# A two-layer diffusion step in float32r pairs: sixteen first places for the modulation pieces, output weights asked for within attention, squares ahead of the fifth piece at the norms, and one more burst in the input projection

## The reference, cut to what matters

```python
sm, cm, gm, sf, cf, gf = split(silu(cond) @ mod_w[l] + mod_b[l], 6)   # per-channel vectors
h = rms_norm(x, g_pre) * (1 + cm) + sm
z = h @ w_in[l]                                   # 2048 -> 4608
o = attention A (6 heads), attention B (6 heads), chunk gMLP (4 groups), all from z
x = x + gm * rms_norm(o @ w_out[l], g_post)       # 2048 -> 2048
h = rms_norm(x, g_pre2) * (1 + cf) + sf
x = x + gf * rms_norm((silu(h @ w_gate) * (h @ w_up)) @ w_down, g_post2)   # 5632 wide
```

## Time and profile before

| | us |
|---|---|
| median of 3 runs | 2378.92 (2378.73 to 2380.59) |
| the profiled execution's own time | 2373.86 |
| its span | 2372.1 |
| PE busy in it | 2276.7 (96%) |
| DVE busy | 1625.2 (69%) |
| ACT busy | 985.3 (42%) |
| POOL busy | 69.2 (3%) |

### The profile page before, as it was taken

The page is one execution under the profiler, slowest core; times in us unless marked ns, Lnnn a source line. Parts: engine busy times, 40 slices in busy tenths (PEclk is TensorE's granted clock), DMA queues, the critical chain, the costliest instruction groups (busy, mean ns, idle before and its releaser), DMA issues.

```text
span 2372.1 us, 27970 instructions
## 1 busy us (share of the span) xinstructions
PE 2276.7 (96%) x10686; PEld 1798.4 (76%) x10686; DVE 1625.2 (69%) x1739; ACT 985.3 (42%) x1277; POOL 69.2 (3%) x97
## 2 busy tenths in 40 slices
PE   4999989999999999999999999899999999999998
PEld 1776766678878888788777887687888888878886
DVE  2555563389888889889887997557888545444455
ACT  2333343364444444334346334347444444433443
POOL 1000120000000000000000101000000000000000
PEclk8999999999999999999999999999999999999999
DMA  8899979868878878788865896865877665666664
GB/s 311 293 348 331 331 246 348 307 209 303 283 254 292 289 263 292 245 282 283 298 225 199 306 320 232 302 200 189 277 261 261 198 194 188 192 179 194 192 219 149
DMA packets 269317, 609.91 MB, mean 257 GB/s; under 512 B 19116, under 2 KB 19296, under 8 KB 267840
## 3 DMA queue, kind: packets, MB, share of 16 engines
q1 hardware_dynamic: 264832, 589.37, 73.1%
q0 software_dynamic: 4352, 18.76, 2.1%
HBM read 603.79 MB, written 5.45 MB: 257 GB/s over the span
## 4 chain that ended last, share of the span: by engine, by line
PE 85%; DMA 7%; DVE 4%; issue 2%; ACT 2%; POOL 1%; SPq 1%; POOLq 0%; DVEq 0%; ACTq 0%
PE bank_B L846 39%; PE bank_A L846 38%; DMA mraw<-in_mod_w 5%; PE bank_X L932 2%; PE bank_M L904 2%; PE bank_M L893 1%; DVE wlo L1441 1%; DMA raw<-in_w_out 1%; ACT whi L1153 1%; PE bank_T L924 1%; DMA raw<-in_w_in 1%; ACT junk L1167 0%; SPq L554 0%; DMA raw<-in_w_gate 0%; DVE x L1549 0%
## 5 line engine op out<-in xcount | busy, mean ns | idle before, releaser
L1441 DVE TENSOR_TENSOR wlo<-raw,whi 128x1024 fp32r<-128x1024 f32 x724 | 880.5, 1222 | 610.8 <-ACT whi L1153 609.8
L1153 ACT CAST whi<-raw 128x1024 fp32r<-128x1024 f32 x724 | 759.1, 1050 | 1176.2 <-PE bank_A L846 554.7
L846 PE MATMUL bank_B<-whi,xt_lo 128*128 128x512 f32 x1104 | 434.1, 393 | 0.7 <-DVE wlo L1441 0.7
L846 PE MATMUL bank_A<-whi,xt_lo 128*128 128x512 f32 x1088 | 428.9, 394 | 3.7 <-DVE xt_lo L1490 3.7
L846 PE MATMUL bank_B<-whi,xt_hi 128*128 128x512 f32 x1104 | 430.5, 390 | 0.0
L846 PE MATMUL bank_B<-wlo,xt_hi 128*128 128x512 f32 x1104 | 430.4, 390 | 0.0
L846 PE MATMUL bank_A<-wlo,xt_hi 128*128 128x512 f32 x1088 | 425.1, 391 | 0.0
L846 PE MATMUL bank_A<-whi,xt_hi 128*128 128x512 f32 x1088 | 424.8, 390 | 0.0
L1462 DVE SCALAR_TENSOR_TENSOR acc<-mraw,cond,acc 128x1024 f32<-128x1024 f32 x300 | 371.1, 1278 | 0.0
L846 PEld LDWEIGHTS bank_A<-whi,xt_lo 128*128 128x128 f32 x1088 | 205.1, 188 | 62.5 <-issue 20.7
L846 PEld LDWEIGHTS bank_B<-whi,xt_lo 128*128 128x128 f32 x1104 | 207.7, 188 | 55.6 <-issue 13.7
(11 more groups left out here) (227 smaller groups left out, 1606.6 us busy)
## 6 DMA issues: line engine op xcount, KB each, us to landing
mraw<-in_mod_w SPq DMA_DIRECT2D x384, 512.0 KB, 5.8
raw<-in_w_gate SPq DMA_DIRECT2D x176, 512.0 KB, 4.4
raw<-in_w_up SPq DMA_DIRECT2D x176, 512.0 KB, 4.4
raw<-in_w_down SPq DMA_DIRECT2D x176, 512.0 KB, 4.7
raw<-in_w_in SPq DMA_DIRECT2D x144, 512.0 KB, 5.6
raw<-in_w_out SPq DMA_DIRECT2D x64, 512.0 KB, 5.5
gate_mix<-gate_rows POOLq DMA_DIRECT2D x4, 1024.0 KB, 8.5
gate_ffn<-gate_rows POOLq DMA_DIRECT2D x4, 1024.0 KB, 8.9
```

Of the source, the lines that this page charges most:

```text
L846: mm = pe.matmul(bank[f"{pair}{s}"][:], xs[:, k, t], w[:, kb, :], start=(k == first and n == 0), stop=(k == (nk - 1 if last is None else l ...
L1153: act.copy(weights(u * UNIT + ph)[0], raw[:, ph % RING]).then_inc(hi_ready, 1)
L1441: dve.tensor_tensor(lo, raw[:, ph % RING], hi.bitcast(F32), ALU.subtract).then_inc(lo_ready, 1)
```

## The change

1. **Sixteen first places.** The first sixteen modulation pieces no longer share the ring of four. Pieces 4 to 15 get places of their own in buffers that are unused at that time (`z`, `qkt`, `hid`, `sil`) and semaphores of their own. SP asks for eight, one piece of `w_in`, the other eight, and three more of `w_in`, without a wait. ACT and DVE split the first `w_in` piece after the first modulation row and the other three after the first blocks of `x`. POOL builds the bias table only after those blocks are ready (`xt_ready` 2), behind the first power.
2. **One burst more in the input projection of layer 0**, behind piece 13 of the last quarter. The bursts of attention in layer 0 move up by one. The output projection of layer 0 has eight, behind pieces 3, 6, 9, 12, 16, 18, 21 and 24.
3. **Weights asked for within attention.** SP asks for `w_out` pieces 4 to 7 behind the fourth of the seven bursts, in both layers. In layer 0 the first four pieces of `w_out` come behind the first burst's pieces.
4. **Norms.** In each turnover but the last, ACT and DVE split the fifth and the sixth piece of the next weight later: ACT takes the fifth behind the squares of `x` and of the last output block, and the sixth behind `pre_high` of block 2. DVE takes the fifth behind the second block's low part instead of ahead of the wait for the power.

```diff
-OUT_MODS = [{2: (-1, range(4, 8))}, {2: (-1, range(4, 8))}]
-OUT_MODS[0].update({q: (h // 2, range(4 * (h % 2), 4 * (h % 2) + 4)) for h, q in enumerate((5, 8, 11, 13, 16, 19, 21, 24))})
+OUT_MODS = [{q: (h // 2, range(4 * (h % 2), 4 * (h % 2) + 4)) for h, q in enumerate((3, 6, 9, 12, 16, 18, 21, 24))},
+            {2: (-1, range(4, 8))}]
-OUT_ENDS = [{2: -1, 24: ND - 1}, {2: -1}]
+OUT_ENDS = [{0: -1, 24: ND - 1}, {2: -1}]
...
+ATT_BURST = [1, 0]
+def att_burst(l, i):
+    m, h = divmod(ATT_BURST[l] + i, 2)
+    return m, range(4 * h, 4 * h + 4)
...
-START_BURSTS = [... ((1, 4, 7, 10, 14), (1, 4, 7, 10, 13, 16), (1, 4, 7, 10, 13, 16), (1, 4, 7)) ...]
+START_BURSTS = [... ((1, 4, 7, 10, 14), (1, 4, 7, 10, 13, 16), (1, 4, 7, 10, 13, 16), (1, 4, 7, 13)) ...]
...
+        def mod_place(q):
+            if not RING <= q < 2 * UNIT:
+                return mraw[:, q % RING]
+            i = q - RING
+            if i >= 10:
+                return (hid, sil)[i - 10][:]
+            t = z[:, i // 4, i % 4 * KB * CH + 4 * P:][:, 0:KB * CH] if i < 8 else qkt[:, 8 * (i - 8):8 * (i - 7), :]...
...   SP, the start
-                mod_chunk(m, 0, range(0, 4), start_chunk(m))
-                if m == 0:
-                    for q in range(LEAD):
-                        start_load(q)
-                mod_chunk(m, 0, range(4, 8), start_chunk(m))
+                mod_chunk(m, 0, range(UNIT), start_chunk(m))
+                for q in range(1, LEAD) if m else range(1):
+                    start_load(q)
...   SP, attention and output projection
-                first_unit(u, w, 0)
-                for step, _, m_att in plan.at[(l, "attention")]:
-                    if step[0] == "mod_first":
-                        mod_chunk(m_att, l)
-                for q in range(LEAD, ND * UNIT):
+                for i in range(7):
+                    if i == 1 - l:
+                        first_unit(u, w, 0)
+                    mi, js = att_burst(l, i)
+                    mod_chunk(m - ND + mi, l, js)
+                    if i == 3:
+                        both(u, w, 0, js=range(LEAD, UNIT))
+                mi, js = OUT_MODS[l][min(OUT_MODS[l])]
+                mod_chunk(m + mi, l, js)
+                for q in range(UNIT, ND * UNIT):
...   POOL: the three loads of the bias table go behind the first power and
+            pool.wait_ge(xt_ready, 2)
...   ACT, turnover
                 split(u, ahead - 1)
-                split(u, ahead)
                 x_squares(0, range(ND))
                 last_square(1)
-                split(u, ahead + 1)
+                split(u, ahead)
...
                 pre_high(l2, w2, 2)
+                split(u, ahead + 1)
...   DVE, turnover
                 split(u, ahead - 1)
                 mean_square(ssx, sq + 11, slice(0, 1))
-                split(u, ahead)
                 dve.wait_ge(rstd_ready, rs + 2)
...
                 pre_low(l2, w2, 1)
+                split(u, ahead)
                 add(1, [2, 3])
```

89 lines of the change are left out of this document (49 added, 40 removed).

## The result

The changed kernel took 2360.86 us (median of 4 runs, 2359.38 to 2367.59) against 2379.6 us for the kernel before (median of 4 runs beside them, 2378.73 to 2380.59). The ratio is 0.993, with a 95% interval of 0.9913 to 0.9948. The profiled execution took 2359.38 us for a span of 2357.6 us. That is 14.5 us less span than before. The medians differ by 18.7 us: the profiled execution of before was 5.7 us faster than the median of these four runs, that of the changed kernel 1.5.

A forecast was written before the change was run, and what follows sets the result against it. PE bounds the kernel, busy 2276.7 of 2372.1 us, leaving 95.4 idle to win. Terms -11.6 + 1.0 + 2.0 - 6.75 - 1.35 - 2.4 = -19.1, off 2378.92, give 2359.8 us; 8-in-10 range 2353 to 2368.

The forecast's parts named there:

- rival A: Input projection: late ring refills, 0.3 us at each of 21 bursts, give back 6.3 us; 2366 us, chance 0.14.
- C: Norms and output projection: DVE's later split hidden (-5.9), refills keep up (-6.6); 2353 us, chance 0.13.
- Start: Up to the first input projection matmul: sixteen pieces under way at once bring it from 52.77 to 41.1, -11.6 us.
- my 20.5: At the start: assumed landing time of `x` in us, between bounds of 19.6 and 32.
- Late by some 5 us: At the start: without moving the bias table behind it, the first power would be late by some 5 us.
- rival E: At the start: SP's queue takes only a few transfers at once, start unchanged; 2371.4 us, chance 0.09 shared with another rival.
- What the start gives back: Input projection: the bias table's traffic now runs beside it, costing +1.0 us, bounds 0 and 8.1.
- One burst more: End of layer 0's input projection: an extra burst's matmuls and switching make the turns into attention 2.0 us later.
- Weights within attention: Attention: four `w_out` pieces fit nearly whole in a DMA gap, 0 us; otherwise up to 2 us per layer.
- Output projection: Layer 0: burst -2.0, shorter burst waits -3.4, turned row's wait -1.35, together -6.75 us.
- Turnovers: Three turnovers: later weight splits bring PE's first turns earlier, partly given back; -1.5, 0 and -0.9, together -2.4 us.
- Layer 1: Output projection there: only the turned row's wait for a late split goes, -1.35 us.

The follow-up runs named there:

- second and third profile of the changed kernel: Reruns of the changed kernel with no edit, beside the kernel before: 2362.62 us (ratio 0.9929) and 2362.1 us (ratio 0.994).
- The table later: Changed kernel with the bias table built only after eight normed blocks of `x` are ready, not two: 2361.49 us, ratio 0.9931 to the kernel before.
- both orders together: Changed kernel with the bias table ahead of the first power and layer 0's `w_out` ahead of attention's first pieces: 2360.3 us, ratio 0.9921 to before.

## Why the prediction was right, and where its steps were not

The total was right: 2359.8 predicted, 2360.86 measured; -19.1 predicted in span and -14.5 in the profiled pair, whose kernel before was 5 us faster than its runs. That it came within 1.1 us is in part luck: the sum holds errors of both signs, and by the spans of the pair it is 4.6 us too large. The forecast's mechanism held at the start, in the output projection and in the turnovers. The steps between them failed, and rivals A and C both came true in part and cancelled.

*Start: right, chain and size.* -12.9 for -11.6. The link that decides was `x` and not the modulation data. `x` took 10.5 us from its issue, though SP stood over a full queue from 5.44 to 16.97. The 1.3 us more are the squares, which began 0.9 before my 20.5, and `mod(1)`, which took 5.5 us and not 6.4. The experiment with the ring of four corrects what the places are for: 4.5 us are theirs, and 7.9 us come with the rest of the change, most likely from what the DMA engines no longer carry ahead of the modulation pieces. "Late by some 5 us" for a table ahead of the power was too much: it costs 2.0 at the start, and there the last modulation pieces were late (0.28 and 0.79 us of waits), not the power. Half of rival E was true as well: SP could not have all of it under way at once: behind the first nine pieces it stood 11.53 us over four issues. That cost nothing, since `mod(1)` never waited for a piece.

By the Trainium skill ("DMA: Bandwidth & Descriptors", queues, rings and completion order) I had estimated a half of 400 GB/s for `x`, with a landing at 21.5; the row says 19.6. The trace agrees with the taking of turns and not with my half: from 13 to 18 us the two queues moved 220 and 222 packets, but those of `x` were four times as large: 1.67 MB for 0.43. The turns are by packet, so a queue of large packets takes most of the bytes. The last step of the bias table is of that kind too: beside it, from 49.9 to 58.5 us, POOL's queue moved 1.17 MB in 80 packets, and SP's 1.64 MB in 849.

*What the start gives back: mis-sized.* Taken as +1.0, bounds 0 and 8.1; measured +4.8 up to burst 20. The step that failed read a mean: "12% of 247 us is 30 us of free DMA time, so it fits as a mean". In the second and third profile of the changed kernel it was +3.9 and +6.3. With the table at the start again the stretch took 221.1 and 222.3 us for 222.1 before, so what is given back hangs on the table's place. This is rival A in part (3.8 us more than forecast, where it had 6.3), but not by its mechanism: the loss is not spread over the bursts. From the first to the third of them it took 25.5 us (48.12 to 73.66) and before 21.4 (60.16 to 81.58); 4.1 of the 4.8 are there, beside the table's copy and just behind it.

*One burst more: mis-sized and incomplete.* Taken as +2.0, measured +6.5. Two paths lead to `z` here, and both are late. PE's own path: the burst costs its 1.92 us of matmuls, then 2.45 of waiting for its own pieces in the middle and 1.6 us for the matmuls behind that wait at half pace (0.43 us each for 0.23; the granted clock of 290 to 294 is 0.65). The other is `w_out`, and there the slack of 9 us that I gave the fourth piece was not: the change itself has SP ask for six modulation pieces ahead of `w_out`, SP stands 13.62 us over them because PE has not yet freed their places, and ACT's splits wait 10.81. From ACT's first split of `w_out` to the turns of `z` it is then 8.5 us, in all three profiles of the changed kernel (298.9 to 307.4, 299.3 to 307.8, 300.6 to 309.1): DVE has two splits to do ahead of each of its last copies of `z`. In the first profile the two paths end together. In the second PE ran at full pace and `z` was no sooner: its turns waited 4.40 us. With `w_out` asked first such a wait is still there, 1.99, so of the 4.40 the late weights are 2.4, and of the first profile's 2.15 next to nothing. I had counted the bytes ahead of `w_out` and not the place in SP's order. The step measured +6.5, +7.2 and +6.7 in the three profiles; with `w_out` asked first it is +4.1 and +4.3.

*Weights within attention: the place was right, the price not.* The empty stretch was filled: a share of 1.05 where it was 0.00. In the whole stage 280 GB/s in 54.2 us are 15.2 MB, where 255 in 51.4 were 13.1: just the four pieces. The stage took 2.8 us more, for which I took 0 and gave 2 as the bound. Burst waits behind the turns of `z` are only 1.2 of that (6.0 for 4.9). How much is the weights' is not shown: with the weights late the stage took 52.4 and 54.0, in the three profiles of the changed kernel 54.0 to 55.0.

*Output projection: right sign, too small.* -10.9 for -6.75. I added up waits of instructions. Bytes give it better: before, the stage moved 321 GB/s in 123.3 us, 39.6 MB. Now eight pieces of 0.524 MB (four of the burst, four of weights) are moved elsewhere, and 315 GB/s in 112.4 us are 35.4 MB. At the rate of before these would take 110.3. This fits a stage that was bound by DMA before and is bound by PE now (108.6 of 112.4 busy, at a clock of 1.00 for 0.97), but it is a fit and not shown. The experiments show that either half alone gives next to nothing (125.1 without the burst moved, 123.1 or 122.1 without the weights moved, 123.3 before). Bytes alone say 116.6 for these, and they moved only 299 to 306 GB/s, so bytes are not the whole account. The rows show the rest as waits of 9.8 us before bursts in the one and 5.35 to 7.63 before a turned row in the others, with slow matmuls behind them (clock 0.96). Why the two edits help each other so much is not settled further than that.

*Turnovers: right.* -1.5, -0.7 and -1.7 for -1.5, 0 and -0.9, with the waits at the places that were named. In the second profile of the changed kernel they were -1.6, 0 and -1.4, in the third -1.5, 0 and -1.6. Putting the old order back cost 1.7 to 2.8 us.

*Layer 1:* the wait of the turned row is gone, as predicted, but no gain is shown. The stretch up to the turnover took 333.8 us for 334.7, and in the other profiles of the changed kernel 335.3 and 334.6. In attention there are 4.9 us of burst waits where there were 4.2.

The general error: I priced each edit where it stands. Up to the first turnover the kernel moves the same 150.5 MB in each of these versions, at 315 GB/s before (478.7 us) and 321 after (469.0). What an edit gives or takes in one stage shows up in another: the extra burst costs 6.5 to 7.2 us ahead of `z` and without it the output projection takes 125.1 us instead of 111.5 to 115.0. The table later, both orders together and the output weights first had `z` 3.6 to 7.2 us earlier than the three profiles of the changed kernel and `t1` 0.9 to 6.5 earlier, and none had a median more than 2 us lower. The table first kept all of its lead up to `t1` (5.7 to 8.8 us earlier) and had 2.9 in the median. So it is not shown that a removed wait comes back in the next stage; a part of these leads is chance, by the spreads above. None of these medians is resolved against the changed kernel, so no version here is shown to beat it; the lowest were 2359.68 and 2360.3.

## What to carry to other kernels

Where DMA is busy for 0.9 of a long stretch, count the bytes that an edit takes out of that stretch and puts where the engines idle, not only the wait that it removes, and read the stages behind it too. A load of another queue with large packets takes more than its share beside a stream of small ones, so choose what it runs beside. Requests go in the order in which the engines that split or copy will reach them, since one late piece holds up all that is queued behind its split. At a start, list what the DMA engines must carry ahead of the last piece that PE needs before buying more buffers: the buffers gave one third of the gain here, and the rest of the change two thirds. And before reading a mark of one profile, look how far it moves in runs whose edit lies behind it.

## What the runs showed of the hardware that was not expected

A wait of PE can cost more than its length. Behind the wait of 2.45 us at the entry into attention the next matmuls of 128x512 came 0.43 us apart and not 0.23, for some 3 us, at a granted clock of 0.65 in 290 to 294 us; in the third profile, behind a wait of 2.11, it was 0.64. But in the second profile, behind a wait of 2.47 at the same place, it was 1.00, and behind waits of 2.63 (at 432.45) and 3.31 (at 1245.36) the pace was the full one as well. The length of the wait alone does not decide.

SP's issues take time of their own when much is asked for: the first nine 512 KB pieces took about 0.5 us each, and the four behind them 11.53 us in all, with no semaphore to wait for. (The 13.62 us for six at the entry into attention are another thing: there SP waits for places, and the issues themselves are short.) Pieces asked for behind the first eight did not delay the 1 MB load of `x` from another queue: 10.5 us from issue to landing in both kernels. In the ring of four, where SP's four pieces had landed by 9 us, the same load took 7.4 us, and the first power ran at 23.03 and not at 26.13.

The two queues were served packet for packet and not byte for byte: 220 packets with 1.67 MB against 222 with 0.43 MB from 13 to 18 us, and 222 with 1.69 against 221 with 0.42 in the kernel before.

POOL's power behind the squares of `x` (128x1) took 1.47 to 1.48 us with a DVE split beside it, in all three turnovers of the old order, and 0.54 to 0.55 without, in all three of the new.
